# A 16-tile part of a down projection done as pairs of seven quarter products instead of plain blocks

## The chip, the cores and the metric

One core of one Trainium2 chip. The metric is the device time of one execution, in microseconds, median of several. The engines: TensorE (PE in the profile, PEld is its weight load), VectorE (DVE), ScalarE (ACT), GpSimd (POOL), and the queues that issue transfers: SyncE's (SPq) and ScalarE's own (ACTq). TensorE's clock is shown as the granted share of its full speed.

## The reference

The kernel is a decoder block over 512 tokens of width 1024 in float32. The part that matters here is its last stage:

```
xn2 = rms_norm(h, norm2_w)
h = h + (silu(xn2 @ w_ffn_gate) * (xn2 @ w_ffn_up)) @ w_ffn_down     # 1024 -> 2816 -> 1024
y = rms_norm(h, final_norm_w)
```

The last matrix product is the down projection. It sums over 2816 = 22 x 128 features; 128 of them are a row tile of `w_ffn_down`.

## The kernel before, in words

**Arithmetic.** Each float32 operand is split in a high part (a copy rounded to the fp32r format, written by ScalarE) and a low part (operand minus high part, by VectorE or GpSimd). A product is three matmuls: high x high, high x low, low x high.

**Blocks.** The plain form (`block_N`) takes 256 rows of a weight (a block of 1 MB): 4 token tiles x 2 column halves x 2 row tiles x 3 = 48 matmuls with the activations as the 128x128 stationary operand and 512 weight columns as the moving one. ScalarE writes `w_hi` (`high`, `down_high`), GpSimd `w_lo` (`low`), and `raw[s]`, `w_hi[s]`, `w_lo[s]` alternate between two slots. The down projection is eleven such blocks; its activations are split beside it (`act_high` on ScalarE, `act_low` on VectorE). The results add up in all eight PSUM banks, and are added to the residual `h` at the very end (`add_half`), followed by the final norm.

**Pairs.** The gate and up projections of the FFN (all but the first 256 features) run as ten pairs (pair 8 to pair 17 in the numbering of the semaphores; seven pairs of an earlier stage are 1 to 7). A pair multiplies the normed activations by two groups of 128 weight columns each. Both operands are cut in four quarters and seven products of quarters (Winograd's form of Strassen's rule) stand for the eight of the plain form. In order: A11, S1, S2, S3, A12, A22, S4. Each is 2 x 4 x 3 = 24 matmuls with a weight quarter stationary and 256 tokens moving, so a pair is 168 matmuls. A11, A12, A22 are plain weight quarters; S1 to S4 are sums of quarters, formed by VectorE in PSUM banks 4 to 7 (`form_s1` to `form_s4`, in `chain` and `diff`, after ScalarE's `a21_copy`). ScalarE writes all high parts, GpSimd the low parts of A11, A12, A22 (L427), VectorE those of S1 to S4 (L1266). On the other side stand quarters of the activations (x11, x21, x22) and four token sums t1 to t4, formed once. The seven results are put together as they come: `take_p1`, `take_c11` on ScalarE (`taken`), `join_u2`, `join_u3`, `join_c22`, `join_c21`, `join_c12` on VectorE (`joined`). For the FFN, `pair_silu` (ScalarE, L942) and `gated_pair` (GpSimd, L483) then write two tiles of `act`, the input of the down projection.

**What sets the order.** Every engine's program is written out by hand, and engines meet only in semaphores. An engine works its list strictly in order. TensorE waits before each product of pair p for its operand's low part (`s_low`, `plain_low`) and for its bank to be free (`taken`, `joined`). The last join of pair p (`join_c12`) stands in VectorE's list behind `form_s2` of pair p+1, and product S1 of pair p+1 waits for it. SyncE's queue loads the weights of pair p+2 (two transfers of 1 MB) once the quarters of pair p have been read (`pair_read`).

**Seven pairs before.** Pairs 1 to 7 (gates and branches) have the same form. In pairs 3 to 6 the activations themselves change, so their quarters and sums are split again between products (`refill`, `refill_t`, `t_low_of`), and in pairs 5 to 7 GpSimd multiplies by the gates (`weighted`, two instructions). The token sums of the first stage were sent through DRAM (`turned_sums`).

Of the kernel before, what the change touches and what calls it, by code (L numbers as in the profile page):

```python
# [30 lines left out]
P = 128  # L31
SEQ = 512
# [30 lines left out]
HT = SEQ // 2  # L63
DOWN_BLKS = KF // 2


B_DOWN = B_FFN + 2
N_BLKS = B_DOWN + DOWN_BLKS
# [4 lines left out]
LAST_PAIR = MERGE_PAIRS + PAIRS  # L73
SKIPPED_MERGE = 2 * MERGE_PAIRS
SKIPPED = SKIPPED_MERGE + 2 * PAIRS
# [15 lines left out]
def build(nc, x, x_t, wstream, w_lr, cols, vbias, lnw, lnb, sgub, sgu_wt, w_gk2, ident_d, causal_d, finalw, out):  # L91
    with ExitStack() as ctx:
# [7 lines left out]
        def at(p, k, o=0):  # L100
# [49 lines left out]
              [sb("rt_b0", 112, [P, 4, HT]), sb("rt_b1", 116, [P, 4, HT])])  # L150
        raw_out = [sb(f"raw_out{s}", 120 + 16 * s, [P, BLK]) for s in range(2)]
# [11 lines left out]
        op_lo = {n: sb(f"{n}_lo", kb + 4, [P, 2, 4, P], F32R) for n, kb in SLOT.items()}  # L163
        sq_junk0 = sb("sq_junk0", 190, [P, D])
# [46 lines left out]

        turned_sums = nc.dram_tensor("turned_sums", (4, P, 4 * HT), F32).ap()
# [6 lines left out]
        diff = acc[:, 6:8, :].rearrange("p a (k n) -> p a k n", k=4)  # L219

# [53 lines left out]
        h0_low = sem("h0_low")  # L274
        vector_scaled, pool_scaled, scalar_scaled, y_stored = (
# [3 lines left out]
        block = ctx.enter_context(nc.Block())  # L279

# [8 lines left out]
        def _(sp):  # L289
# [86 lines left out]
            with sp.Fori(B_DOWN // 2 + 1, N_BLKS // 2) as i:  # L376
                for s in range(2):
                    sp.wait_ge(hi_ready, i * 2 + (s - 1))
                    sp.wait_ge(lo_ready, i * 2 + (s - 1))
                    sp.dma_start(raw[s][:, :], wstream[bass.ds(i * 2 + (SKIPPED + s), 1)].rearrange("a p n -> (a p) n")  # L380
                                 ).then_inc(raw_landed[s], 16)
# [19 lines left out]
        def _(pool):  # L401
# [23 lines left out]
            def plain(name, c, ks, cs, high):  # L425
                pool.wait_ge(op_high, high)
                pool.tensor_tensor(op_lo[name][:, :, :, :], wp[c][:, :, ks, cs], op_hi[name][:, :, :, :], ALU.subtract  # L427
                                   ).then_inc(plain_low, 1)

            def a11_low(c, high):  # L430
                plain("A11", c, slice(0, 4), slice(0, P), high)

            def a12_low(c, high):
                plain("A12", c, slice(4, 8), slice(0, P), high)

            def a22_low(c, high):
                plain("A22", c, slice(4, 8), slice(P, 2 * P), high)
# [48 lines left out]
            def pair(p, c, first=False, last=False):  # L486

                a12_low(c, at(p, 7, (5 if first else 4) - 7))
                if not first:
                    gated_pair((p[0], p[1] - 1))  # L490
                a22_low(c, at(p, 7, 6 - 7))
                if not last:
                    a11_low(1 - c, at(p, 7, 1))
# [32 lines left out]
            with pool.Fori(1, PAIRS // 2) as i:  # L526
                for c in (1, 0):
                    pair((i, MERGE_PAIRS + 1 - c), c)
            pair((None, LAST_PAIR), 1, last=True)
            pool.wait_ge(product_done, 7 * LAST_PAIR - 3)  # L530
            low(B_DOWN, 0, 8 * B_DOWN)
            gated_pair((None, LAST_PAIR))
            low(B_DOWN + 1, 1, 8 * B_DOWN)
            with pool.Fori(B_DOWN // 2 + 1, N_BLKS // 2) as i:
                for s in range(2):
                    low(i * 2 + s, s, i * 16)
# [14 lines left out]
        def _(a):  # L551
# [1582 lines left out]
```

## Time and profile before

| | |
|---|---|
| median of 3 runs | 826.28 us (825.98 to 826.77) |
| the profiled execution | 826.09 us, of which 824.4 us are its span |
| TensorE busy | 99% of the span, granted clock 0.998 |
| VectorE, ScalarE, GpSimd busy | 62%, 50%, 47% |

The span runs from the first to the last instruction. A matmul's duration in the profile is its way through the pipeline, and several overlap; the time that one adds to a stream is the distance between two starts. Shares of busy time are means over stages with different limits.

### The profile page before, as it was taken

Reading aid. Unit: us, or ns where it says so; the run is one execution under the profiler, and the core shown is the slowest. Engines: PE = TensorE matmul, PEld = TensorE weight load, DVE = VectorE, ACT = ScalarE, POOL = GpSimd, SP = SyncE. Lnnn points to the kernel's source line nnn. Section 1 sums busy time; section 2 is a strip of 40 time slices with the busy share of each in tenths; the row PEclk is TensorE's granted clock in tenths of the full one; section 3 lists DMA queues with packets and bytes.
Section 4 is the critical chain, followed back from the end, with each engine's and each line's share of the span. In section 5 each row is a group of like instructions: output and inputs, shape, how many; then the busy total and the mean of one; then the engine's idle time right before and its main releaser. Section 6 shows DMA issues by size and latency. Waiting matters only on the chain.

```text
span 824.4 us, 12835 instructions
## 1 busy us (share of the span) xinstructions
PE 816.0 (99%) x5224; PEld 742.7 (90%) x5224; DVE 509.7 (62%) x506; ACT 414.9 (50%) x464; POOL 383.7 (47%) x129
## 2 busy tenths in 40 slices
PE   9999999999999999999999999999999999999996
PEld 7888888888888899999998899999999999888885
DVE  6477377374675867888863387666666666244444
ACT  4523446665675645856432674555544445122234
POOL 4445424424224533568954433444444445544443
PEclk9999999999999999999999999999999999999999
DMA  9842422121123353333252305433333321322212
GB/s 339 309 163 103 157 98 103 53 101 66 56 89 127 96 181 103 103 104 103 103 194 117 103 2 164 144 102 102 102 102 102 102 102 52 127 102 79 81 44 102
DMA packets 20615, 94.36 MB, mean 114 GB/s; under 512 B 1889, under 2 KB 2273, under 8 KB 15585
## 3 DMA queue, kind: packets, MB, share of 16 engines
q1 hardware_dynamic: 17456, 83.92, 29.6%
q10 hardware_dynamic: 3120, 9.90, 3.1%
q8 instruction: 28, 0.46, 0.2%
q14 instruction: 11, 0.08, 0.0%
HBM read 89.62 MB, written 4.19 MB: 114 GB/s over the span
## 4 chain that ended last, share of the span: by engine, by line
PE 99%; DVE 0%; ACT 0%; issue 0%; ACTq 0%
PE acc L1847 14%; PE acc L1849 14%; PE acc L1850 14%; PE acc L1641 9%; PE acc L1643 9%; PE acc L1642 9%; PE acc L1624 7%; PE acc L1625 6%; PE acc L1626 6%; PE acc L1667 3%; PE acc L1761 1%; PE acc L1800 1%; PE acc L1805 1%; PE acc L1792 1%; PE acc L1657 1%; PE acc L1974 0%
## 5 line engine op out<-in xcount | busy, mean ns | idle before, releaser
L406 POOL TENSOR_TENSOR w_lo<-raw,w_hi 128x2048 fp32r<-128x2048 f32 x34 | 158.8, 4671 | 219.6 <-ACT w_hi L560 219.6
L427 POOL TENSOR_TENSOR A_lo<-wp,A_hi 128x1024 fp32r<-128x1024 f32 x51 | 126.2, 2474 | 143.1 <-ACT A_hi L732 143.1
L560 ACT ACTIVATE w_hi<-raw 128x2048 fp32r<-128x2048 f32 x34 | 64.9, 1912 | 125.6 <-PE acc L1643 111.3
L1849 PE MATMUL acc<-xt_lo,A_hi 128*128 128x256 f32 x408 | 115.5, 283 | 0.0
L1850 PE MATMUL acc<-xt_hi,A_lo 128*128 128x256 f32 x408 | 115.5, 283 | 0.0
L1847 PE MATMUL acc<-xt_hi,A_hi 128*128 128x256 f32 x408 | 115.5, 283 | 0.0
L745 ACT ACTIVATE S_hi<-acc 128x1024 fp32r<-128x1024 f32 x68 | 68.1, 1024 | 88.6 <-PE acc L1850 55.6
L1266 DVE TENSOR_TENSOR S_lo<-acc,S_hi 128x1024 fp32r<-128x1024 f32 x68 | 81.8, 1220 | 18.6 <-ACT S_hi L745 18.6
L1624 PE MATMUL acc<-xt_hi,w_hi 128*128 128x512 f32 (+1 forms) x240 | 92.5, 385 | 0.0
L1626 PE MATMUL acc<-xt_hi,w_lo 128*128 128x512 f32 (+1 forms) x240 | 91.7, 382 | 0.0
L1625 PE MATMUL acc<-xt_lo,w_hi 128*128 128x512 f32 (+1 forms) x240 | 91.7, 382 | 0.0
L1527 DVE TENSOR_TENSOR al<-act,ah 128x1024 fp32r<-128x1024 f32 x11 | 48.2, 4385 | 63.0 <-ACT ah L957 63.0
L1849 PEld LDWEIGHTS acc<-xt_lo,A_hi 128*128 128x128 f32 x408 | 78.3, 192 | 0.0
L1847 PEld LDWEIGHTS acc<-xt_hi,A_hi 128*128 128x128 f32 x408 | 78.3, 192 | 0.0
L1850 PEld LDWEIGHTS acc<-xt_hi,A_lo 128*128 128x128 f32 x408 | 78.3, 192 | 0.0
L1641 PE MATMUL acc<-w_hi,ah 128*128 128x512 f32 x176 | 68.5, 389 | 0.0
L1642 PE MATMUL acc<-w_lo,ah 128*128 128x512 f32 x176 | 68.5, 389 | 0.0
L1643 PE MATMUL acc<-w_hi,al 128*128 128x512 f32 x176 | 68.5, 389 | 0.0
L1847 PE MATMUL acc<-tb_hi,S_hi 128*128 128x256 f32 x240 | 67.9, 283 | 0.0
L1849 PE MATMUL acc<-tb_lo,S_hi 128*128 128x256 f32 x240 | 67.9, 283 | 0.0
L1850 PE MATMUL acc<-tb_hi,S_lo 128*128 128x256 f32 x240 | 67.9, 283 | 0.0
L732 ACT ACTIVATE A_hi<-wp 128x1024 fp32r<-128x1024 f32 x51 | 53.8, 1055 | 18.7 <-PE acc L1850 18.7
(284 smaller groups left out, 2030.2 us busy)
## 6 DMA issues: line engine op xcount, KB each, us to landing
raw<-wstream SPq DMA_DIRECT2D x34, 1024.0 KB, 4.8
wp<-wstream SPq DMA_DIRECT2D x34, 1024.0 KB, 8.3
turned_sums<-tx ACTq DMA_DIRECT2D x4, 512.0 KB, 3.8
raw_out<-wstream SPq DMA_DIRECT2D x2, 1024.0 KB, 5.8
raw_ffn<-wstream SPq DMA_DIRECT2D x2, 1024.0 KB, 9.1
h<-x ACTq DMA_DIRECT2D x1, 2048.0 KB, 14.1
xw<-x_t SPq DMA_DIRECT2D x3, 512.0 KB, 10.1
mt_raw<-turned_sums SPq DMA_DIRECT2D x3, 512.0 KB, 4.1
```

The lines of the kernel that those rows point to most:

```text
L406: pool.tensor_tensor(w_lo[s][:, :], raw[s][:, :], w_hi[s][:, :], ALU.subtract).then_inc(lo_ready, 1)
L427: pool.tensor_tensor(op_lo[name][:, :, :, :], wp[c][:, :, ks, cs], op_hi[name][:, :, :, :], ALU.subtract).then_inc(plain_low, 1)
L1266: v.tensor_tensor(op_lo[name][:, :, :, :], src, op_hi[name][:, :, :, :], ALU.subtract).then_inc(s_low, 1)
L1624: pe.matmul(dst, wh[:, k, cs], rh[:, k, ts], start=(k == 0), stop=False)
L1625: pe.matmul(dst, wh[:, k, cs], rl[:, k, ts], start=False, stop=False)
L1626: last = pe.matmul(dst, wl[:, k, cs], rh[:, k, ts], start=False, stop=(k == KD - 1))
L1641: pe.matmul(dst, lh[:, k, ts], wh[:, k, cs], start=(first and k == 0), stop=False)
L1642: pe.matmul(dst, lh[:, k, ts], wl[:, k, cs], start=False, stop=False)
L1643: mm = pe.matmul(dst, ll[:, k, ts], wh[:, k, cs], start=False, stop=(last and k == 1))
L1847: pe.matmul(dst, wh[:, g, k, :], x[0][:, k, :], start=(start and g == 0 and k == 0), stop=False, skip_group_check=True)
L1849: pe.matmul(dst, wh[:, g, k, :], x[1][:, k, :], start=False, stop=False, skip_group_check=True)
L1850: mm = pe.matmul(dst, wl[:, g, k, :], x[0][:, k, :], start=False, stop=(k == 3), skip_group_check=True)
```

## The change

The first 16 of the 22 row tiles of the down projection (act tiles 0 to 15) become four pairs, 18 to 21, ahead of three remaining plain blocks. Two pairs share a chunk of eight row tiles: pairs 18 and 19 take chunk 0, each for one half of the 1024 output columns, pairs 20 and 21 chunk 1. Here the activations are stationary (128x128) and a quarter of the weight is moving, 256 columns wide (`down_product`).

- The token sums of each chunk (four of 512 KB) are formed by VectorE during pairs 13 to 16 (`act_sums`), stored to DRAM by ScalarE's queue (`store_sums`), and read back by SyncE's queue during pair 17 and pair 19 (`sum_back`) into the place that their low parts will take. They lie meanwhile in tiles of `act` that pairs 15 to 17 will fill, so GpSimd waits for the stores (`t_stored`) ahead of its lists for pairs 16 and 17.
- During pairs 17/18 and 19/20 the split quarters and sums are replaced by those of the next chunk: seven instructions on ScalarE (`act_x`, `act_t`), five on GpSimd (`act_x`, `act_t_low`) and two on VectorE (`act_t_low_of`), of 1024 elements a partition each.
- The four joined quarters of a down pair go to `dq`, and GpSimd adds them to `h` (`add_pair`, two instructions a pair).
- Weight loads of a down pair are four transfers of 512 KB in pieces of 2 KB.
- The loops over pairs are written out from pair 13 on.

```diff
+DOWN_CHUNKS = 2
+DOWN_PAIRS = 2 * DOWN_CHUNKS
+K_PLAIN = KD * DOWN_CHUNKS
...
+PLAIN_BLKS = DOWN_BLKS - K_PLAIN // 2
...
-LAST_PAIR = MERGE_PAIRS + PAIRS
+LAST_FFN = MERGE_PAIRS + PAIRS
+LAST_PAIR = LAST_FFN + DOWN_PAIRS
...
+SUM_TILES = (20, 18, 16, 18), (18, 20, 20, 18)
+SUM_ORDER = (0, 1, 2, 3), (0, 2, 1, 3)
+FIRST_SUMS = 6
...
-            for q in range(2, PAIRS):
-                pair_read((None, MERGE_PAIRS + q - 1))
-                pair_weights(wstream[W_FFN + 2 * q + 2:W_FFN + 2 * q + 4], q % 2)
+            def sum_back(p, n):
+                m = (p - LAST_FFN) // 2
+                dst = sum_raw[n][:, :, :].rearrange("p k t -> p (k t)") if n < 3 else sum_raw[n]
+                src = down_sums[4 * m + n] if n < 3 else down_sums[4 * m + n].rearrange("p (k t) -> p k t", k=4)
+                sp.wait_ge(t_stored, A_STORED + 64 * (m + 1))
+                sp.wait_ge(product_done, 7 * p + (2, 3, 4, 6)[n] - 7)
+                sp.dma_start(dst, src).then_inc(sum_landed[n], 16)
+
+            def down_weights(p):
+                c, m, n = p % 2, (p - LAST_FFN - 1) // 2, (p - LAST_FFN - 1) % 2
+                for hf, landed in enumerate((k1_landed[c], k2_landed[c])):
+                    for j in range(2):
+                        k = 4 * hf + 2 * j
+                        sp.dma_start(wd[c][:, k:k + 2, :], wstream[W_DOWN + 4 * m + k // 2].rearrange("p (k n) -> p k n", k=2)
+                                     [:, :, n * HALF:(n + 1) * HALF]).then_inc(landed, 16)
+
+            for p in range(MERGE_PAIRS + 3, LAST_PAIR + 1):
+                ends = p - 2 in (LAST_FFN, LAST_FFN + 2)
+                if ends:
+                    for n in range(3):
+                        sum_back(p - 2, n)
+                pair_read((None, p - 2))
+                if p <= LAST_FFN:
+                    w = W_FFN + 2 * (p - MERGE_PAIRS)
+                    pair_weights(wstream[w:w + 2], p % 2)
+                else:
+                    down_weights(p)
+                if ends:
+                    sum_back(p - 2, 3)
             pair_read((None, LAST_PAIR - 1))
             for s in range(2):
                 sp.dma_start(raw[s][:, :], wstream[B_DOWN + SKIPPED + s]).then_inc(raw_landed[s], 16)
...
+            def add_pair(p, halves=(0, 1)):
+
+                pool.wait_ge(joined, 5 * p)
+                pool.wait_ge(taken, 2 * p)
+                n = (p - LAST_FFN - 1) % 2
+                for i in halves:
+                    c0 = n * HALF + i * HT
+                    quarter = h[:, :, c0:c0 + HT]
+                    pool.tensor_tensor(quarter, quarter, dq[(p - LAST_FFN - 1) % 2][:, 2 * i:2 * i + 2, :, :].rearrange("p j t c -> p (j t) c"),
+                                       ALU.add).then_inc(h_added, 1)
...
+            for p in range(MERGE_PAIRS + FIRST_SUMS, LAST_FFN + 1):
+                if p - 1 >= MERGE_PAIRS + 8:
+                    pool.wait_ge(t_stored, A_STORED + 64 * (p - 1 - MERGE_PAIRS - 7))
+                pair((None, p), p % 2)
+            for p in range(LAST_FFN + 1, LAST_PAIR + 1):
+                down_pair(p)
             pool.wait_ge(product_done, 7 * LAST_PAIR - 3)
...
+            def store_sums(q):
+                m = (q - FIRST_SUMS) // 2
+                for i in range(2):
+                    i += 2 * ((q - FIRST_SUMS) % 2)
+                    n = SUM_ORDER[m][i]
+                    a.wait_ge(t_formed, A_FORMED + 4 * m + i + 1)
+                    a.dma_start(down_sums[4 * m + n], act_sum[SUM_TILES[m][n]][:, :, :].rearrange("p k t -> p (k t)")
+                                ).then_inc(t_stored, 16)
+
+            def act_x(p, product, m, ks, ts):
+                a.wait_ge(product_done, 7 * p + product - 7)
+                k = KD * m + ks.start
+                a.activation(xt_hi[:, ks, ts], act[:, k:k + 4, ts], ACT.Copy).then_inc(refill_high, 1)
+
+            def act_t(p, n):
+                a.wait_ge(sum_landed[n], 16 * ((p - LAST_FFN) // 2 + 1))
+                a.wait_ge(product_done, 7 * p + (2, 3, 4, 6)[n] - 7)
+                dst = tb_hi[n][:, :, :] if n < 3 else xt_hi[:, 0:4, HT:SEQ]
+                a.activation(dst, sum_raw[n][:, :, :], ACT.Copy).then_inc(t_high, 1)
...
+            def act_sums(q):
+
+                m = (q - FIRST_SUMS) // 2
+                x11, x12, x21, x22 = act_quarters(m)
+                t1, t2, t3, t4 = (act_sum[k][:, :, :] for k in SUM_TILES[m])
+                if q == FIRST_SUMS:
+                    v.wait_ge(pair_ready, 3)
+                    v.tensor_tensor(t1, x12, x11, ALU.subtract).then_inc(t_formed, 1)
+                    v.wait_ge(t_formed, A_FORMED + 1)
+                    v.tensor_tensor(t2, x22, t1, ALU.subtract).then_inc(t_formed, 1)
...
+                if q == FIRST_SUMS + 3:
+                    v.wait_ge(t_formed, A_FORMED + 5)
+                    v.wait_ge(t_stored, A_STORED + 64 + 32)
+                    v.tensor_tensor(t2, x22, t1, ALU.subtract).then_inc(t_formed, 1)
+                    v.wait_ge(t_formed, A_FORMED + 7)
+                    v.tensor_tensor(t4, x21, t2, ALU.subtract).then_inc(t_formed, 1)
...
+            def down_product(name, x, b, start):
+
+                wh, wl = row_hi[name], row_lo[name]
+                for t in range(2):
+                    dst = bank[b][:, t * HT:(t + 1) * HT]
+                    ts = slice(t * P, (t + 1) * P)
+                    for k in range(4):
+                        pe.matmul(dst, x[0][:, k, ts], wh[:, k, :], start=(start and t == 0 and k == 0), stop=False,
+                                  skip_group_check=True)
+                        pe.matmul(dst, x[0][:, k, ts], wl[:, k, :], start=False, stop=False, skip_group_check=True)
+                        mm = pe.matmul(dst, x[1][:, k, ts], wh[:, k, :], start=False, stop=(k == 3),
+                                       skip_group_check=True)
+                mm.then_inc(product_done, 1)
```

On GpSimd, before: its rows for pair 17 (the last pair then; A_lo is a plain quarter's low part, act the gated tiles of pair 16 and then 17) and the start of the blocks.

```order
L427 TENSOR_TENSOR A_lo<-wp_120,A_hi 128x1024 [waits op_high]
L483 TENSOR_TENSOR act<-silp,cq 128x1024 [waits silp_ready]
L427 TENSOR_TENSOR A_lo<-wp_120,A_hi 128x1024 [waits op_high]
L406 TENSOR_TENSOR w_lo_53<-raw_49,w_hi_51 128x2048 [waits hi_ready,raw_landed0,product_done]
L483 TENSOR_TENSOR act<-silp,cq 128x1024 [waits silp_ready]
```

On GpSimd, after: its rows for pair 17 (the first six) and pair 18 (A_row_lo is a plain quarter of a down pair, xt_lo and tb_lo are quarters and sums of the activations).

```order
L490 TENSOR_TENSOR A_lo<-wp_129,A_hi 128x1024 [waits op_high,t_stored]
L552 TENSOR_TENSOR xt_lo<-act,xt_hi 128x4x256 [waits refill_high]
L546 TENSOR_TENSOR act<-silp,cq 128x1024 [waits silp_ready]
L490 TENSOR_TENSOR A_lo<-wp_129,A_hi 128x1024 [waits op_high]
L490 TENSOR_TENSOR A_row_lo<-wd_144,A_row_hi 128x1024 [waits op_high]
L557 TENSOR_TENSOR tb_lo_127<-sum_raw_111,tb_hi_124 128x1024 [waits t_high]
L490 TENSOR_TENSOR A_row_lo<-wd_144,A_row_hi 128x1024 [waits op_high]
L552 TENSOR_TENSOR xt_lo<-act,xt_hi 128x4x256 [waits refill_high]
L546 TENSOR_TENSOR act<-silp,cq 128x1024 [waits silp_ready,t_stored]
```

Pair 17 had three instructions of 1024 elements here and now has six, and the first of them waits for the stores too.

On VectorE, before: its rows for pair 17 (acc is chain or diff, u and cq are joins, al the activations' low part for the blocks).

```order
L1259 TENSOR_TENSOR acc<-acc,wp_120 128x1024
L1508 TENSOR_TENSOR cq<-acc,u_82 128x512 [waits product_done]
...
L1505 TENSOR_TENSOR u_83<-acc,u_82 128x512 [waits joined,product_done]
L1508 TENSOR_TENSOR cq<-acc,u_83 128x512 [waits joined,pair_ready]
L1527 TENSOR_TENSOR al_146<-act,ah_144 128x1024 [waits ah_ready]
L1508 TENSOR_TENSOR cq<-acc,u_82 128x512 [waits product_done] x2
```

On VectorE, after: its rows from `join_c22` of pair 17 to `form_s2` of pair 18.

```order
L1703 TENSOR_TENSOR cq<-acc,u_83 128x512 [waits joined,pair_ready]
L1754 TENSOR_TENSOR tb_lo_125<-sum_raw_109,tb_hi_122 128x1024 [waits t_high]
L1447 TENSOR_TENSOR acc<-wd_144,acc 128x1024
L1754 TENSOR_TENSOR tb_lo_126<-sum_raw_110,tb_hi_123 128x1024 [waits t_high]
L1703 TENSOR_TENSOR cq<-acc,u_82 128x512 [waits product_done]
L1461 TENSOR_TENSOR S_row_lo<-acc,S_row_hi 128x1024 [waits op_high]
L1703 TENSOR_TENSOR cq<-acc,u_82 128x512 [waits product_done,s_low]
L1451 TENSOR_TENSOR acc<-acc,wd_144 128x1024
```

Two splits of sums (L1754) stand ahead of `join_c21`, and `join_c12` of pair 17 now stands ahead of `form_s2`, behind the low part of S1.

## Rows read from the trace of the kernel before

**Rows 1.** The page: busy time by engine, and the chain that ended last.

```profile
PE 816.0 (99%) x5224; PEld 742.7 (90%) x5224; DVE 509.7 (62%) x506; ACT 414.9 (50%) x464; POOL 383.7 (47%) x129
...
PE 99%; DVE 0%; ACT 0%; issue 0%; ACTq 0%
```

**Rows 2.** Timeline of PE (start us, duration us): first of pair 8, pair 17, blocks; last.

```profile
496.44 0.28 PE L1847 MATMUL acc<-xt_hi,A_hi 128*128 128x256 f32 x1
...
677.88 0.28 PE L1847 MATMUL acc<-xt_hi,A_hi 128*128 128x256 f32 x1
...
698.03 0.40 PE L1641 MATMUL acc<-w_hi,ah 128*128 128x512 f32 x1
...
817.52 0.39 PE L1643 MATMUL acc<-w_hi,al 128*128 128x512 f32 x1
```

**Rows 3.** Timeline of PE, an earlier stage: weights stationary, 512 columns moving.

```profile
284.49 0.39 PE L1625 MATMUL acc<-xt_lo,w_hi 128*128 128x512 f32 x1
284.72 0.39 PE L1626 MATMUL acc<-xt_hi,w_lo 128*128 128x512 f32 x1
```

**Rows 4.** Timeline of DVE, pairs 16 and 17.

```profile
671.59 1.22 DVE L1256 TENSOR_TENSOR acc<-wp,acc 128x1024 f32<-128x1024 f32 x1
675.20 0.69 DVE L1508 TENSOR_TENSOR cq<-acc,u 128x512 f32<-128x512 f32 x1 [2.39 <-PE acc L1850]
...
679.74 0.68 DVE L1508 TENSOR_TENSOR cq<-acc,u 128x512 f32<-128x512 f32 x1
...
690.84 0.69 DVE L1508 TENSOR_TENSOR cq<-acc,u 128x512 f32<-128x512 f32 x1
691.45 4.93 DVE L1527 TENSOR_TENSOR al<-act,ah 128x1024 fp32r<-128x1024 f32 x1
```

**Rows 5.** Timeline of POOL, pair 17.

```profile
678.24 2.41 POOL L427 TENSOR_TENSOR A_lo<-wp,A_hi 128x1024 fp32r<-128x1024 f32 x1 [6.20 <-ACT A_hi L732]
682.58 2.42 POOL L483 TENSOR_TENSOR act<-silp,cq 128x1024 f32<-128x1024 f32 x1 [1.93 <-ACT silp L942]
...
690.66 4.63 POOL L406 TENSOR_TENSOR w_lo<-raw,w_hi 128x2048 fp32r<-128x2048 f32 x1 [3.27 <-ACT w_hi L560]
```

**Rows 6.** Timeline of ACT, end of pair 16 and pair 17.

```profile
677.10 1.06 ACT L732 ACTIVATE A_hi<-wp 128x1024 fp32r<-128x1024 f32 x1
679.94 1.02 ACT L745 ACTIVATE S_hi<-acc 128x1024 fp32r<-128x1024 f32 x1 [1.78 <-DVE acc L1259]
680.96 0.60 ACT L948 ACTIVATE p<-acc 128x512 f32<-128x512 f32 x1
681.45 1.05 ACT L942 ACTIVATE silp<-cq 128x1024 f32<-128x1024 f32 x1
```

**Rows 7.** Timeline of POOL, pair 6, where activations are replaced.

```profile
388.58 2.42 POOL L453 TENSOR_TENSOR xt_lo<-yb,xt_hi 128x1024 fp32r<-128x1024 f32 x1
390.93 5.79 POOL L449 TENSOR_TENSOR sg_a<-mcq,sg_a 128x1024 f32<-128x1024 f32 x2
396.66 3.41 POOL L427 TENSOR_TENSOR A_lo<-wp,A_hi 128x1024 fp32r<-128x1024 f32 x1
```

**Rows 8.** Timeline of DVE in pair 6.

```profile
395.38 2.42 DVE L1316 TENSOR_TENSOR xt_lo<-yb,xt_hi 128x1024 fp32r<-128x1024 f32 x1
```

**Rows 9.** Transfers: issues (count, KB each, median us to landing), then sums stored and read.

```profile
wp<-wstream SPq DMA_DIRECT2D x34, 1024.0 KB, 8.3
turned_sums<-tx ACTq DMA_DIRECT2D x4, 512.0 KB, 3.8
mt_raw<-turned_sums SPq DMA_DIRECT2D x3, 512.0 KB, 4.1
xn_in<-x SPq DMA_DIRECT2D x2, 512.0 KB, 12.5
...
DMA to landing us min/median/max: 2.6/4.0/7.1
```

**Rows 10.** Timeline of SPq in pair 15: the issue of the weights of pair 17.

```profile
647.52 0.88 SPq L316 DMA_DIRECT2D wp<-wstream  x2
```

More of the change, by code:

```diff
@@ L969, in pair @@
                 a22_high(c, n)
+                a.wait_ge(product_done, at(p, 7, 3 - 7))
+                s_high("S4", chain, at(p, 4))
+                a.wait_ge(s_low, at(p, 4, 1 - 4))
+                a21_copy(1 - c, nn, rows)
+                a11_high(1 - c, nn, rows)
+                if renewed is not None:
+                    act_t(p[1], 0)
+                take_c11(p, first)
+                if renewed is not None:
+                    act_t(p[1], 1)
+                    act_x(p[1], 5, renewed, slice(4, 8), slice(0, HT))
+                    act_t(p[1], 2)
@@ new lines, in pair @@
+                a.wait_ge(product_done, at(p, 7, 6 - 7))
+                s_high("S1", chain, at(p, 4, 1), rows)
+                s_high("S3", diff, at(p, 4, 2), rows)
+                a12_high(1 - c, nn, rows)
+                if q is not None and q < PAIRS:
+                    store_sums(q)
+            def store_sums(q):
[6 more added lines that the diff above has]
+                                ).then_inc(t_stored, 16)
@@ L1550, in pair @@
                 join_c22(p, first)
+                if q == PAIRS:
+                    act_t_low_of(0, 0)
+                form_s3(1 - c, rows)
+                if q == PAIRS:
+                    act_t_low_of(0, 1)
+                elif q is not None:
+                    act_sums(q)
+                join_c21(p)
+                s_low_of("S1", chain, at(p, 7, 2), rows)
+                if q != PAIRS:
+                    s_low_of("S3", diff, at(p, 7, 3), rows)
+                v.wait_ge(s_low, at(p, 4, 1))
@@ L1551, in pair @@
                 if last:
                     act_low(1, 1)
-                if not last:
-                    form_s3(1 - c)
-                join_c21(p)
-                if not last:
-                    s_low_of("S1", chain, at(p, 7, 2))
-                    s_low_of("S3", diff, at(p, 7, 3))
-                    v.wait_ge(s_low, at(p, 4, 1))
+                else:
+                    form_s3(1 - c, True)
+                if ends:
+                    act_t_low_of(m + 1, 1)
+                down_c21(p)
@@ L1561, in _ @@
+                if not last:
+                    s_low_of("S1", chain, 7 * p + 2, True)
+                    if not ends:
+                        s_low_of("S3", diff, 7 * p + 3, True)
+                    v.wait_ge(s_low, 4 * p + 1)
             pair((None, MERGE_PAIRS + 1), 0, 16, first=True)
-            with v.Fori(1, PAIRS // 2) as i:
+            with v.Fori(1, (FIRST_SUMS - 1) // 2 + 1) as i:
                 pair((i, MERGE_PAIRS), 1, i * 16 + 16)
                 pair((i, MERGE_PAIRS + 1), 0, i * 16 + 16)
-            pair((None, LAST_PAIR), 1, 0, last=True)
@@ L1566, in _ @@
-            join_c12((None, LAST_PAIR))
+            for q in range(FIRST_SUMS, PAIRS + 1):
+                pair((None, MERGE_PAIRS + q), (q - 1) % 2, 16 * (q // 2 + 1) + 16 * (q == PAIRS), q=q)
+            for p in range(LAST_FFN + 1, LAST_PAIR + 1):
+                down_pair(p)
+            down_c12(LAST_PAIR)
             act_low(2, 0)
-            with v.Fori(0, 4) as i:
-                for s in range(2):
-                    act_low(i * 2 + (3 + s), 1 - s)
             v.wait_ge(fw_landed, 16)
+            v.wait_ge(h_added, 2 * DOWN_PAIRS)
@@ L2036, in down @@
+            for p in range(LAST_FFN + 1, LAST_PAIR + 1):
+                down_pair(p)
             def down(m, s, first=False, last=False):
```

345 lines of the change are left out of this document (263 added, 82 removed).

## The prediction, made before the changed kernel was run

> **What bounds the kernel now.** I read the page's busy times first: PE is busy in 99% of the span, and the chain that ended last lies on PE for 99% [rows 1]. Next the timeline of PE, for the distance between starts. Ten pairs of 168 matmuls run from 496.44 to 698.03 us [rows 2]: 201.59 us, so 20.159 us a pair, 2.880 us a product and 0.1200 us for a matmul of 256 columns. The 528 matmuls of the down projection start from 698.03 to 817.52 [rows 2]: 527 steps in 119.49 us, 0.2267 us for one of 512 columns. Neither stretch leaves room for a wait, so every other engine is hidden here, and the stage is worth what its matmuls are worth. Then I read VectorE, GpSimd and ScalarE inside pair 17, since this is the work that has to stay hidden. Below, "+x" is x us after a pair's first matmul (677.88 for pair 17).
>
> **Matmuls.** Removed: eight blocks of 48 = 384 matmuls of 512 columns, 384 x 0.2267 = 87.1 us. Added: four pairs of 168 = 672 matmuls of 256 columns, 672 x 0.1200 = 80.6 us. The difference is 6.4 us, not the 10.9 us that an eighth of 87.1 would be, because two short matmuls take 0.0133 us longer than one long one (2 x 0.1200 - 0.2267). What is new is which operand stands still. With the weights stationary and 512 columns moving the starts lie 0.23 us apart [rows 3], as with the activations stationary in the blocks [rows 2]; so the side does not matter at 512 columns, and I take 0.1200 at 256. Bounds: 0.1133 (half of the long one), a gain of 10.9 us, and 0.1333 (the fixed 0.0133 us of each matmul twice over), a loss of 2.5 us. Neither end has a row that supports it.
>
> The first row also tests a rule. The rows give 0.1200 and 0.2267 us. The Trainium skill, page "TensorE: Matmul & The Clock Gate", section "Back-to-back issue gap", gives for one stream at the full clock N columns over 2.4 GHz plus about 2.5 ns: 109.2 and 215.8 ns. By the page the sum would be an estimated 82.9 - 73.4 = 9.5 us of gain; this trace doesn't agree with it at either width (11 ns more each), and the measurement decides.
>
> **Work that is added behind TensorE.** One VectorE instruction of 1024 elements costs 1.22 us [rows 4], one of GpSimd 2.41 [rows 5], one of ScalarE 1.05 [rows 6].
> - Token sums, pairs 13 to 16: two VectorE instructions a pair, behind `form_s3`. In pair 16 that ends at 672.81, and the next instruction starts at 675.20 after 2.39 us idle [rows 4]; two take 2.4. Nothing is moved.
> - Pair 17, GpSimd: six instructions of 1024 elements (14.5 us) in 20.2. Their order matters. A12's low part starts at +0.36 today [rows 5], x11's at about +4.7 (ScalarE is done with `take_p1` at +3.6 and needs 1.05 for its high part [rows 6]), then `gated_pair` and A22's low part: +11.9. Product A22 starts at +14.40. The slack is 2.5 us.
> - But the first of them now waits for two stores. ScalarE issues them beside or behind the copy of 677.10 [rows 6], at -0.8 to +0.3. Landing was 2.6 to 7.1 us, median 3.8 for a store [rows 9]. So X, the time at which GpSimd may begin, is +1.8 to +7.7, likeliest +3.4 to +4.5. Four instructions in a row end at X + 9.6, so TensorE waits for A22 only if X is over 4.8: 0 to 2.9 us, and at the likeliest X nothing.
> - Pair 19, GpSimd: x11 at +4.7, `add_pair` twice, A22: four instructions in a row, +14.3 against +14.40. This is the tightest place. A precedent is pair 6: four instructions from 388.58 end at 400.07 [rows 7], with seven in the pair, and no wait of PE on it. I take 0.1, from nothing to 1.2 (one more instruction of VectorE ahead of it).
> - Pair 18 carries seven instructions (16.9 us) and its A22 and last refill have over 0.9 us each; pairs 20 and 21 carry less before product A22.
> - VectorE, pairs 17 and 19: two splits of sums (2.4 us) between `join_c22` (start 690.84, +12.96 [rows 4]) and `join_c21` (+17.3). With `form_s3` that is 3.7 us from +13.6: +17.3. Nothing is lost if they run at once; the lock below decides.
> - ScalarE: 3 to 4 extra instructions in pair 17 and 19, in idle time; S1's high part moves from +17.4 to about +17.9, its low part to about +20.1; product S1 of the next pair needs it at +23.04.
> - `join_c12` of pairs 17 and 19 ahead of `form_s2`: it comes earlier than the +1.86 to +2.54 of today [rows 4], S2's low part follows at about +5; S2 starts at +5.76.
> - Transfers. SyncE issues weights at 647.52, +10.0 of pair 15 [rows 10], and they land in 8.3 us [rows 9]; needed is the first half at about +9.9 of the next pair, 20 us later. The queue now waits for products 2 to 4 (+11.5 at the latest) first, and the 512 KB of sums land in 4.1 us [rows 9] at about +9.9, +12.8, +15.7; ScalarE takes them at +11.9, +15, +17. Late by 2 us they still cost nothing. The weights of pair 19 are issued latest (+14.5 of pair 17, behind A22's low part); their pieces of 2 KB are new, and if these took twice the 8.3 us they would land at +31.1 where +30.1 is wanted: 1 us, at most.
> - Last three blocks: GpSimd has the first `w_lo` by +18.3 of pair 21, the second by +26.6 (needed +31), the third by +38 (needed +42). The final `add_half` sees every addition long done. The tail stays.
>
> Sum: -6.4 for matmuls, +0.2 for waits of a tenth at two or three places: -6.2. The profiled execution (826.09, 1.7 over its span of 824.4) would become 819.9; its 826.09 is 0.2 below the median of 826.28, so the median becomes **820.1 us**.
>
> **Rivals.**
> 1. The lock between VectorE and GpSimd delays a join (20%). A VectorE instruction with both inputs in SBUF took 4.93 us at 691.45, and ended 1.1 us after GpSimd's of 690.66 (4.63 us) [rows 4, 5]; in pair 6 such a one took 2.42 and GpSimd's next 3.41 instead of 2.41 [rows 7, 8]. So whoever comes second waits, for up to 2.4 us (VectorE) or 1.1 (GpSimd). In pair 17 with X between about 3.6 and 4.0 each split of a sum meets a GpSimd instruction that has just begun: `join_c21` ends at +22.1, S1's low part at +23.3, `join_c12` at +24.0 where TensorE wants it at +23.04, and S2 is 0.7 late behind it: 1.7 us. Twice that (pair 19 too), or with X late as well, makes 1.5 to 4.5 us: 821.6 to 824.6. For it: all three places are within 1 us of their limit. Against it: pairs 3 to 6 had the same forms, and PE's stream kept its pace.
>    The Trainium skill, page "SBUF — State Buffer", section "SBUF: two separate sides", says that the shared pair of ports is an exclusive lock for a whole instruction, taken by VectorE with two SBUF inputs against a reading GpSimd. By that rule the trace agrees (4.93 for 1.22).
> 2. Slower than before: the sums come back late (4%). `act_t` for t3 stands in ScalarE's list ahead of S1, S3 and A12 of the next pair, and everything waits if the load is late. Issued at +11.6, it must land by about +19.2 (7.6 us) for `join_c12` to stay in time, and each further us is lost twice (pairs 17 and 19). Slower by 0.2% needs 8.1 us of loss, so 11.7 us of landing each. For it: 512 KB once took 12.5 [rows 9]. Against it: that was at the start with the queues full; sums took 2.6 to 7.1 [rows 9].
> 3. A matmul with 256 weight columns moving has a longer step than 0.1200 (3%): from 0.1296 us on the gain is gone, and at 0.1333 it is 828.8. Against it: rows 2 and 3 at 512 columns.
> 4. Matmuls at 0.1133, or a pace that is better with weights moving (2%): 815.4 at best.
> 5. Several losses of 1 and 2 together, 4.8 to 8.0 us (4%): 824.9 to 828, no change that can be told.
>
> **How the numbers follow.** Forecast 67% (819.4 to 821.5), rival 1 20%, rival 2 4%, rival 3 3%, rival 4 2%, rest 4%. The range for 8 in 10 takes the forecast's own range and rival 1 up to 3.5 us of waits: 819.0 to 823.6. Faster by over 0.2% (below 824.6) is 67 + 20 + 2 = 89%, less 1 for rival 1's upper end: 88%. Within 0.2% (about what runs of this kernel can tell): rival 5 and half of rival 3, with that 1: 6%. Slower: 6%.
>
> **What would show it.** PE's starts 0.1200 us apart in the 672 new matmuls, and 80.6 to 81.5 us from the first of pair 18 to the first block's; three blocks in 32.6 us. If I am wrong, PE's timeline has gaps in pair 17 ahead of A22 (a late store), at S1 or S2 of pairs 18 and 20 (the lock, with VectorE's L1754 at 2 us or more each), or at A22 of pair 19. Pairs 8 to 16 keep 20.16 us. If the gap between starts is itself longer, rival 3 holds; if ScalarE idles ahead of its splits of sums on a DMA for microseconds, rival 2.

## The result and the profile after

The changed kernel takes 820.24 us in the median of six executions (819.95 to 820.39), the kernel before beside it 826.14 (825.97 to 826.77, six): a ratio of 0.9926, 95% interval 0.9917 to 0.9936. Forecast were 820.1 in a range of 819.0 to 823.6. The profiled execution took 820.24, of which 818.5 are its span, at a granted clock of 0.999.

The page, busy times and chain that ended last; these two lines answer to [rows 1].

```profile
PE 810.3 (99%) x5512; PEld 752.0 (92%) x5512; DVE 539.6 (66%) x562; ACT 440.8 (54%) x502; POOL 421.0 (51%) x151
...
PE 99%; DVE 0%; ACT 0%; issue 0%; ACTq 0%
```

TensorE has 288 matmuls more (672 for 384) and is busy 5.7 us less. VectorE has 30 us more work, ScalarE 26, GpSimd 37, and the chain still lies on TensorE.

The timeline of PE answers to [rows 2]: first matmul of pairs 8, 17 and 18, the two on either side of the only gap, first and last of the blocks.

```profile
496.89 0.28 PE L2137 MATMUL acc<-xt_hi,A_hi 128*128 128x256 f32 x1
...
678.33 0.28 PE L2137 MATMUL acc<-xt_hi,A_hi 128*128 128x256 f32 x1
...
698.49 0.28 PE L2333 MATMUL acc<-A_row_hi,xt_hi 128*128 128x256 f32 x1
...
733.04 0.34 PE L2333 MATMUL acc<-A_row_hi,xt_hi 128*128 128x256 f32 x1
733.23 0.28 PE L2335 MATMUL acc<-A_row_lo,xt_hi 128*128 128x256 f32 x1
...
779.18 0.40 PE L1931 MATMUL acc<-w_hi,ah 128*128 128x512 f32 x1
...
811.62 0.39 PE L1933 MATMUL acc<-w_hi,al 128*128 128x512 f32 x1
```

From pair 8 to pair 17 there are 181.44 us in both traces. Pairs 18 to 21 take 779.18 - 698.49 = 80.69 us, which is 672 x 0.1200 (80.64) and one gap: between 733.04 and 733.23 lie 0.19 us instead of 0.12. (A step is the distance between two starts.) The three blocks have 143 steps in 32.44 us, 0.2269 each. From pair 8's first matmul to the last matmul there are 314.73 us, and there were 321.08 [rows 2]: 6.35 less. The last matmul is 6.9 us from the span's end in both. Pair 8 starts 0.45 us later than in the trace before; what lies ahead of it is unchanged, and in the other traces below that start lies anywhere from 496.51 to 497.19. So 6.35 is the effect in the two traces. The 5.90 between the two medians is less, and the scatter of the start can account for it, which is argued and not shown; the four variants below without a gap worth naming came out 6.1 to 6.4 under the kernel before beside them.

GpSimd in pairs 17, 18 and 19, answering to [rows 5].

```profile
680.19 2.42 POOL L490 TENSOR_TENSOR A_lo<-wp,A_hi 128x1024 fp32r<-128x1024 f32 x1 [7.79 <-DMA down_sums<-act_sum]
...
687.76 2.41 POOL L490 TENSOR_TENSOR A_lo<-wp,A_hi 128x1024 fp32r<-128x1024 f32 x1
...
725.81 4.76 POOL L567 TENSOR_TENSOR h<-h,dq 128x1024 f32<-128x1024 f32 x2
730.53 5.78 POOL L490 TENSOR_TENSOR A_row_lo<-wd,A_row_hi 128x1024 fp32r<-128x1024 f32 x2
```

In pair 17 GpSimd was held by the store, as the releaser says, and began at 680.19, +1.86 (678.24, +0.36, before [rows 5]). A22's low part ends at 690.17, +11.8, with 2.6 us in hand. In pair 19 the row of 730.53 holds two splits: the first, of 2.4 us, ends at about 732.9 = +14.3, and that is the gap of 0.07 us at the product A22, whose first matmuls with the low part stand in the rows of PE above.

Why the store was early: VectorE forming the last two sums, then ScalarE and its queue at the end of pair 16.

```profile
673.35 1.22 DVE L1748 TENSOR_TENSOR act_sum<-act,act_sum 128x1024 f32<-128x1024 f32 x1
674.61 1.22 DVE L1750 TENSOR_TENSOR act_sum<-act,act_sum 128x1024 f32<-128x1024 f32 x1
...
675.65 1.02 ACT L861 ACTIVATE S_hi<-acc 128x1024 fp32r<-128x1024 f32 x1 [2.28 <-PE acc L2140]
675.66 0.81 ACTq L1114 DMA_DIRECT2D down_sums<-act_sum  x2
...
677.47 1.06 ACT L846 ACTIVATE A_hi<-wp 128x1024 fp32r<-128x1024 f32 x1
```

In ScalarE's list the stores stand behind three copies, of which 675.65 is the first and 677.47 the last. They were issued as the first began, at -2.7, instead of the -0.8 to +0.3 of the forecast. The first of the two had its own wait met at 674.57, when its sum was formed, and still went out only at 675.66, when the copy at the head of the list had its product from TensorE. So the stores were held by the waits ahead of them in the list, and not by the copies' work (experiment 4 shows the same once more). That an engine works its list strictly in order, as said above, holds for a transfer only in this sense.

VectorE in pairs 17, 18 and 19, answering to [rows 4]: the splits of sums are L1754, the joins L1703 and L1798.

```profile
692.02 1.64 DVE L1754 TENSOR_TENSOR tb_lo<-sum_raw,tb_hi 128x1024 fp32r<-128x1024 f32 x1
...
694.72 1.21 DVE L1754 TENSOR_TENSOR tb_lo<-sum_raw,tb_hi 128x1024 fp32r<-128x1024 f32 x1
...
697.31 1.23 DVE L1461 TENSOR_TENSOR S_row_lo<-acc,S_row_hi 128x1024 fp32r<-128x1024 f32 x1 [0.78 <-ACT S_row_hi L861]
698.76 0.69 DVE L1703 TENSOR_TENSOR cq<-acc,u 128x512 f32<-128x512 f32 x1 [0.22 <-PE acc L2140]
...
732.34 1.69 DVE L1754 TENSOR_TENSOR tb_lo<-sum_raw,tb_hi 128x1024 fp32r<-128x1024 f32 x1
...
735.09 2.31 DVE L1754 TENSOR_TENSOR tb_lo<-sum_raw,tb_hi 128x1024 fp32r<-128x1024 f32 x1
...
739.16 0.69 DVE L1798 TENSOR_TENSOR dq<-acc,u 128x512 f32<-128x512 f32 x1
```

`join_c12` starts at 698.76 (+20.4) and 739.16 (+20.5); TensorE wants it done by +23.04. Three of the four splits took 1.64 to 2.31 us where 1.21 is the time of one alone. Each of the three ended 1.1 us after the GpSimd instruction beside it (at 692.58, 732.9 and 736.3), as in [rows 4, 5], and the reserve took it up.

Transfers on the page, and the reads of the sums and the weights' issue in pair 17 on SyncE's queue; they answer to [rows 9, 10].

```profile
wd<-wstream SPq DMA_DIRECT2D x16, 512.0 KB, 6.4
down_sums<-act_sum ACTq DMA_DIRECT2D x8, 512.0 KB, 3.4
sum_raw<-down_sums SPq DMA_DIRECT2D x8, 512.0 KB, 3.3
```
```profile
684.33 6.08 SPq L419 DMA_DIRECT2D sum_raw<-down_sums  x3
690.51 2.53 SPq L426 DMA_DIRECT2D wd<-wstream  x4
```

The 2 KB pieces cost TensorE nothing: a `wd` load lands in 6.4 us. (512 KB of sums land in 3.3, but they are not issued four in a row, so what the pieces cost the transfer is not shown.) Each issues in about 0.6 us, so the last of the four leaves at about 692.5, and the first half is wanted at about 708.4 (+30.1 of pair 17).

### The profile page after: what moved, and what is told of

It reads as the page before. It is cut to its first block, busy times and chain, and to the rows that moved or that the text cites. A ratio compares the mean times of both kernels' runs of the same rounds, so it can differ in the third digit from the quotient of the medians.

```text
span 818.5 us, 13393 instructions
## 1 busy us (share of the span) xinstructions
PE 810.3 (99%) x5512; PEld 752.0 (92%) x5512; DVE 539.6 (66%) x562; ACT 440.8 (54%) x502; POOL 421.0 (51%) x151
## 4 chain that ended last, share of the span: by engine, by line
PE 99%; DVE 0%; ACT 0%; issue 0%; ACTq 0%
PE acc L2137 14%; PE acc L2139 14%; PE acc L2140 14%; PE acc L1914 7%; PE acc L1916 6%; PE acc L1915 6%; PE acc L1933 6%; PE acc L1931 6%; PE acc L1932 6%; PE acc L2333 3%; PE acc L2335 3%; PE acc L2336 3%; PE acc L1957 3%; PE acc L2051 1%; PE acc L2090 1%; PE acc L2095 1%
## 5 line engine op out<-in xcount | busy, mean ns | idle before, releaser
L469 POOL TENSOR_TENSOR w_lo<-raw,w_hi 128x2048 fp32r<-128x2048 f32 x26 | 122.2, 4701 | 165.6 <-ACT w_hi L674 165.6
L861 ACT ACTIVATE S_hi<-acc 128x1024 fp32r<-128x1024 f32 x68 | 68.1, 1024 | 89.5 <-PE acc L2140 56.3
L674 ACT ACTIVATE w_hi<-raw 128x2048 fp32r<-128x2048 f32 x26 | 49.6, 1910 | 68.3 <-PE acc L1933 53.6
L846 ACT ACTIVATE A_hi<-wp 128x1024 fp32r<-128x1024 f32 x51 | 53.8, 1055 | 17.9 <-PE acc L2140 17.9
L1916 PEld LDWEIGHTS acc<-xt_hi,w_lo 128*128 128x128 f32 x240 | 45.1, 188 | 8.8
L1914 PEld LDWEIGHTS acc<-xt_hi,w_hi 128*128 128x128 f32 x240 | 45.1, 188 | 8.7
L1915 PEld LDWEIGHTS acc<-xt_lo,w_hi 128*128 128x128 f32 x240 | 45.1, 188 | 8.5
L2137 PE MATMUL acc<-mt_hi,S_hi 128*128 128x256 f32 x168 | 47.7, 284 | 0.0
```

Source lines behind the costliest of these rows:

```text
L469: pool.tensor_tensor(w_lo[s][:, :], raw[s][:, :], w_hi[s][:, :], ALU.subtract).then_inc(lo_ready, 1)
L674: a.activation(w_hi[s][:, :], raw[s][:, :], ACT.Copy).then_inc(hi_ready, 1)
L846: a.activation(high_of(name, rows), weights_of(name, c, rows), ACT.Copy).then_inc(op_high, 1)
L861: a.activation(high_of(name, rows), src, ACT.Copy).then_inc(op_high, 1)
L1914: pe.matmul(dst, wh[:, k, cs], rh[:, k, ts], start=(k == 0), stop=False)
L1915: pe.matmul(dst, wh[:, k, cs], rl[:, k, ts], start=False, stop=False)
```

## The experiments

Ten kernels, in three groups, each group on one chip beside the kernel before. The forecast had said what a matmul costs, where the added work has no slack, and how much it has elsewhere; each is tried alone. All compute the reference in full.

**1. One chunk of the two** (one_chunk): two pairs and seven plain blocks.

```
-DOWN_CHUNKS = 2
+DOWN_CHUNKS = 1
```

The rest of its edit, not shown, is what follows from it: four more blocks in each engine's loops, and in pair 19 both additions to `h` ahead of A22's low part as before, with no exchange of activations there.

> Half the change: only the first eight row tiles as two pairs (18 and 19), seven plain blocks behind them. If the gain is matmuls alone (192 of 512 columns at 0.2267 us out, 336 of 256 at 0.1200 in), it is half of the whole change's: -3.2 us on the kernel before, 822.9 us. If the whole change also lost something at its second exchange of activations (pairs 19 and 20) or gained from elsewhere, the half is not half: under 822.5 or over 823.5.

Timeline of PE, first matmul of pair 8 and the last one.

```profile
496.64 0.28 PE L2139 MATMUL acc<-xt_hi,A_hi 128*128 128x256 f32 x1
...
814.52 0.39 PE L1935 MATMUL acc<-w_hi,al 128*128 128x512 f32 x1
```

317.88 us for 321.08: 3.20 less, half of 6.40, and no gap. In the trace the gain belongs to the pairs, in proportion. The median is 823.67 (823.12 to 823.90, six), ratio 0.9968 [0.9956, 0.9981], 2.5 us less. That is over the 823.5 above which the expectation called the half not a half. The profiled execution, 823.12, was the shortest of the six and comes out 3.0 under the kernel before; the three longest (823.74 to 823.90) have a mean granted clock of 0.997, the others 0.998 to 0.999. What they lost no trace shows, so the half is shown for the matmuls and not for the median.

**2. The kernel before with blocks of short matmuls** (blocks256): each matmul of the eleven down blocks as two of 256 columns, nothing else.

```
-                block_N(s, ah[s], al[s], first, last, free)
+                narrow_block(s, ah[s], al[s], first, last, free)
```

`narrow_block`, not shown, is `block_N` with an inner loop over the two 256-column parts of each 512 columns.

> The kernel before, with each matmul of the down projection's eleven blocks cut in two of 256 columns (1056 instead of 528), activations stationary. If the step is 0.0133 us plus 256 columns at the full clock, 1056 x 0.1200 = 126.7 us for 119.7: +7.0 us, 833.1 us. By a fixed part of 2.5 ns (the Trainium skill's page on TensorE) an estimated +1.3 us. If activations stationary with narrow weights are slower than 0.1200, more than +7.

Timeline of PE: first of the blocks, last.

```profile
698.12 0.28 PE L2046 MATMUL acc<-w_hi,ah 128*128 128x256 f32 x1
...
824.72 0.28 PE L2049 MATMUL acc<-w_hi,al 128*128 128x256 f32 x1
```

Median 833.17 (832.97 to 833.19, four), ratio 1.0082 [1.0065, 1.0099]; 1055 steps in 126.60 us, 0.1200 each, 7.1 us more than the 119.49 of 527 long steps [rows 2]. So a short matmul with the activations stationary and the weights moving costs 0.1200 as well, and the 0.0133 us by which two short ones exceed a long one is what separates the gain of 6.4 from the 10.9 of an eighth. The Trainium skill's rule that the forecast weighed ("TensorE: Matmul & The Clock Gate", "Back-to-back issue gap"; the section calls it the gap of an isolated matmul) would make this about 528 x (2 x 109.2 - 215.8) = 1.4 us, an estimate from the page; the measurement says 7.1.

**3. The stores behind the copies** (store_after_copy): ScalarE issues pair 16's two stores only when the last copy of that pair is done.

```
+                    if q == PAIRS - 1:
+                        a.wait_ge(op_high, 7 * LAST_FFN - 3)
```

> The changed kernel; the last two stores of sums wait for A12's copy of pair 17 to end, so GpSimd starts its list of pair 17 some 2.9 us later, at about +4.8 instead of +1.96. Four instructions of 2.4 us end at +14.35; TensorE wants A22 at +14.40. Theory (slack 2.8 us): 0 to +0.1 us, 820.2 to 820.3. If the lock with VectorE bites in this position: +1 to +2.

Timeline of GpSimd, pair 17.

```profile
682.46 2.41 POOL L490 TENSOR_TENSOR A_lo<-wp,A_hi 128x1024 fp32r<-128x1024 f32 x1 [10.21 <-DMA down_sums<-act_sum]
...
691.94 3.39 POOL L490 TENSOR_TENSOR A_row_lo<-wd,A_row_hi 128x1024 fp32r<-128x1024 f32 x1
```

GpSimd starts at +4.3, about 2.4 us later than in the changed kernel and within the forecast's likeliest +3.4 to +4.5; +4.8 was expected of this run. A22's low part ends at 691.97; the next split, behind it, takes 3.39 us for 2.41 beside VectorE's. TensorE has no gap, not even in pair 19, whose list is unchanged: the 0.07 us there are as small as what differs from trace to trace. 820.0 us (819.87 to 820.28, four), 0.9924 [0.9907, 0.9940].

**4. The stores still later** (store_after_p1): issued behind `take_p1` of pair 17.

```
+                if q == PAIRS:
+                    store_sums(PAIRS - 1)
...
-                if q is not None and q < PAIRS:
+                if q is not None and q < PAIRS - 1:
                     store_sums(q)
```

> The changed kernel; these two stores come behind take_p1 of pair 17, so GpSimd starts at about +8.2. Theory (each us past +4.8 stops TensorE for one): A22's low part at +17.8, +3.4 us, 823.6 us, in one gap of PE in front of product A22 of pair 17. If the list of pair 17 had other slack: under +2. If the lock adds to it at the following join: over +4.5.

Timelines of ScalarE and its queue, GpSimd and PE in pair 17 (the copy at 681.41 is `take_p1`).

```profile
681.41 0.60 ACT L1064 ACTIVATE p<-acc 128x512 f32<-128x512 f32 x1
681.42 0.81 ACTq L1116 DMA_DIRECT2D down_sums<-act_sum  x2
```
```profile
685.44 2.40 POOL L490 TENSOR_TENSOR A_lo<-wp,A_hi 128x1024 fp32r<-128x1024 f32 x1 [13.01 <-DMA down_sums<-act_sum]
```
```profile
692.61 0.28 PE L2142 MATMUL acc<-xt_hi,A_lo 128*128 128x256 f32 x1
695.05 0.38 PE L2139 MATMUL acc<-xt_hi,A_hi 128*128 128x256 f32 x1 [2.16 <-POOL A_lo L490]
```

GpSimd may begin at +7.1; the forecast's slack ended at +4.8, which makes 2.3 us, and the gap ahead of A22 is 695.05 - 692.61 - 0.12 = 2.32. The start of +8.2 and the loss of 3.4 that were expected of this run were too much, for the same reason as in the forecast: the stores were issued as `take_p1` began and not when it was done. Median 823.2 (822.41 to 824.33, six), 0.9966 [0.9953, 0.9978]; the profiled execution took 822.63.

**5 and 6. The sums read back one product later, and two** (sums_1_later, sums_2_later).

```
-                sp.wait_ge(product_done, 7 * p + (2, 3, 4, 6)[n] - 7)
+                sp.wait_ge(product_done, 7 * p + (3, 4, 5, 7)[n] - 7)
```

That is sums_1_later; sums_2_later has `(4, 5, 6, 8)[n]` in its place.

> The changed kernel; each read of a sum from DRAM waits for one product more (2.88 us later). ScalarE takes t3's sum about 1 us later, S1's low part and the join behind it still come in time. Theory (transfers have slack): no change, 820.2 +- 0.2. If the round trip through DRAM is what TensorE nearly waits for: +1 to +5.

> The changed kernel; each read of a sum waits for two products more (5.76 us later). Worked out: t3 lands at +20.7, S1's low part at +23.95, the join of C12 at +24.6 where +23.04 is wanted (1.6 us), S2's low part 0.6 us late behind it: 2.2 us in each of pairs 17/18 and 19/20, +4.4 us, 824.6 us. If only the landing mattered and the list behind it did not: 0.

One product later costs nothing: 820.0 (819.94 to 820.42, four), 0.9924 [0.9908, 0.9941]. Two products later: 825.23 (824.50 to 826.66, ten), 0.9988 [0.9979, 0.9998]. Timelines of PE, DVE and ACT at the first of its four gaps (the last row is the copy of t3's sum).

```profile
700.89 0.28 PE L2336 MATMUL acc<-A_row_hi,xt_lo 128*128 128x256 f32 x1
702.73 0.35 PE L2333 MATMUL acc<-S_row_hi,tb_hi 128*128 128x256 f32 x1 [1.56 <-DVE S_row_lo L1461]
```
```profile
700.68 1.23 DVE L1461 TENSOR_TENSOR S_row_lo<-acc,S_row_hi 128x1024 fp32r<-128x1024 f32 x1 [1.88 <-ACT S_row_hi L861]
```
```profile
698.67 1.06 ACT L1126 ACTIVATE tb_hi<-sum_raw 128x1024 fp32r<-128x1024 f32 x1 [0.78 <-DMA sum_raw<-down_sums]
```

1.72 us at S1 and 0.52 at S2 in pair 18, 1.88 and 0.54 in pair 20, 5.0 in all with the first steps behind them; 1.6, 0.6 and 4.4 in all were expected. TensorE waits for S1's low part and then for the join behind it: the copies of the sums stand ahead of S1's copy in ScalarE's list. A delay of 5.76 us cost 2.5 a chunk, so the slack of the reads is about 3.3 us.

**7 and 8. One more GpSimd instruction in pair 19, and in pair 20** (extra19, extra20).

```
             def act_x(n, m, ks, ts):
                 pool.wait_ge(refill_high, A_REFILL + n)
+                if n == 4:
+                    pool.tensor_tensor(silp[:, :, :], xt_hi[:, 0:4, 0:HT], xt_hi[:, 0:4, 0:HT], ALU.subtract)
```

That is extra19; extra20 has `n == 5`. The result goes to memory that nobody reads.

> The changed kernel with one more GpSimd instruction of 1024 elements (2.41 us, into unused memory) in pair 19 ahead of the additions to h. Theory: the list of pair 19 has no slack, so TensorE waits 2.3 us before product A22: 822.5 us. If the wait of 0.07 us seen there came from elsewhere: 820.2.

> The same instruction in pair 20, whose list reaches A22 with 4.9 us to spare. Theory: no change, 820.2 +- 0.2. If GpSimd's total load in this stage sets the pace: +1 to +2.4.

In pair 20 it costs nothing (820.15, 820.01 to 820.69, four). In pair 19 it costs 4.1 us, where 2.3 were expected: 824.37 (822.96 to 824.82, seven), 0.9971 [0.9959, 0.9982]. Timelines of GpSimd, VectorE and PE in pair 19 of extra19.

```profile
723.75 1.89 POOL L552 TENSOR_TENSOR silp<-xt_hi 128x1024 f32<-128x1024 f32 x1 [2.10 <-ACT xt_hi L1122]
...
732.67 6.72 POOL L490 TENSOR_TENSOR A_row_lo<-wd,A_row_hi 128x1024 fp32r<-128x1024 f32 x2
```
```profile
732.64 1.22 DVE L1756 TENSOR_TENSOR tb_lo<-sum_raw,tb_hi 128x1024 fp32r<-128x1024 f32 x1
```
```profile
733.23 0.28 PE L2338 MATMUL acc<-A_row_hi,xt_lo 128*128 128x256 f32 x1
736.12 0.39 PE L2335 MATMUL acc<-A_row_hi,xt_hi 128*128 128x256 f32 x1 [2.61 <-POOL A_row_lo L490]
```

The gap is 2.77 us: 0.07 and the 1.89, and 0.8 more, because VectorE's split began at 732.64, a moment ahead of GpSimd's of 732.67, which was over only at about 736.0. That is rival 1's lock, with a price, at the place that has no slack. The rest of the 4.1 us is not a wait. Stretches of PE in extra19: us, then busy us and count of PE, PEld, DVE, ACT and POOL, granted clock, share of DMA, GB/s.

```profile
733.30:736.10 2.80, 0.21 (x2) 0.01 (x1) 2.68 (x3) 2.55 (x4) 2.80 (x2) 1.00 0.01 4
736.10:737.60 1.50, 1.48 (x12) 1.48 (x13) 1.05 (x1) 0.88 (x1) 1.50 (x1) 1.00 0.11 16
737.60:741.10 3.50, 3.50 (x19) 3.50 (x19) 0.61 (x1) 0.61 (x1) 3.50 (x2) 0.51 0.89 301
741.10:750.00 8.90, 8.90 (x76) 8.90 (x76) 6.71 (x7) 4.37 (x6) 5.41 (x3) 1.00 0.50 173
```

After the gap TensorE ran 1.5 us at full clock, then 3.5 us at a granted 0.51, the level of 1.2 GHz: steps of 0.214 us, about 1.5 us lost.

**9. Half of that instruction** (extra19_half): 512 elements instead of 1024, in pair 19.

> Pair 19 gets a GpSimd instruction half as long as in extra19 (512 elements instead of 1024, about 1.0 us instead of 1.89) in the same place ahead of A22's low part; everything is still computed, the extra instruction writes memory that nobody reads. In the changed kernel TensorE waits 0.07 us there. My theory: the wait becomes 0.07 + 1.0 = 1.1 us, or about 2.1 if VectorE's split of a sum takes its turn first, as it did in extra19, and the clock stays at its full level because the wait is shorter than the 2.8 us after which it fell: 821.2 to 822.3 us, all executions within 0.3 us of each other. Rival: any wait of a microsecond or more brings the half clock, so some executions show 15 steps of 0.214 us behind the wait and are 1.5 us longer (822.7 to 823.8). Second rival: the half clock in extra19 had nothing to do with the wait; then it is missing here and the times lie close, which by itself does not tell this one from my theory.

Timelines of GpSimd and PE in pair 19.

```profile
723.53 1.04 POOL L552 TENSOR_TENSOR silp<-xt_hi 128x512 f32<-128x512 f32 x1 [2.10 <-ACT xt_hi L1122]
```
```profile
733.01 0.28 PE L2338 MATMUL acc<-A_row_hi,xt_lo 128*128 128x256 f32 x1
734.09 0.39 PE L2335 MATMUL acc<-A_row_hi,xt_hi 128*128 128x256 f32 x1 [0.80 <-POOL A_row_lo L490]
```

1.04 us of GpSimd make a gap of 0.96 and 0.10 on the next step, so nothing hides it. Here VectorE's split did not come first. All steps behind the gap are 0.120 us. 821.28 us (820.89 to 821.46, four), 1.0 above the changed kernel, 0.9939 [0.9922, 0.9955]; the four lie 0.6 apart, where 0.3 was expected.

**10. One addition moved behind A22** (add_split19): in pair 19 the second half of pair 18's quarter is added to `h` behind A22's low part.

```
-                    add_pair(p - 1)
+                    add_pair(p - 1, (0,))
                     a22_low(c, 7 * p - 1, rows=True)
+                    add_pair(p - 1, (1,))
```

> Nothing is left out. In pair 19 the second half of the addition of pair 18's quarter to h is done behind A22's low part instead of ahead of it, so that low part starts 2.4 us earlier. The wait of 0.07 us of TensorE at A22 of pair 19 should vanish, and pairs 18 to 21 take 80.64 us from the first matmul of pair 18 to the block's, the pure 672 steps of 0.1200. Time 820.1 to 820.2, which the median can't tell from 820.24. Rival: the order is now such that the half addition, later, meets VectorE's splits of sums, and join_c12 or A11's low part comes late: a gap of 0.5 to 1.5 us at S1 or S2 of pair 20.

Timelines of PE (first matmul of pair 18, first of the blocks) and of GpSimd (A22's low part in pair 19).

```profile
698.11 0.28 PE L2334 MATMUL acc<-A_row_hi,xt_hi 128*128 128x256 f32 x1
...
778.75 0.40 PE L1932 MATMUL acc<-w_hi,ah 128*128 128x512 f32 x1
```
```profile
727.81 2.41 POOL L490 TENSOR_TENSOR A_row_lo<-wd,A_row_hi 128x1024 fp32r<-128x1024 f32 x1
```

80.64 us, the bare 672 steps, and no gap from pair 8 to the end. A22's low part ends at 730.22, 2.8 us ahead of its product. 819.91 us (819.79 to 820.32, four), 0.9925 [0.9908, 0.9941]: the place with no slack is gone, for a gain that the median can't tell.

## Why the prediction was right

The sum holds in its trace: forecast were -6.4 for matmuls and +0.2 for waits, measured -6.42 and +0.07.

- **Matmuls: right.** 672 steps of 0.1200 (pairs 18 to 21), 0.2269 in the blocks. That the operands change sides costs nothing (experiment 2), and in the trace half the pairs give half the gain (experiment 1). Rivals 3 and 4 are out.
- **Pair 19: right to a tenth.** Forecast was a low part at +14.3 and a wait of 0.1; it came at +14.3, with 0.07. Experiments 7 to 10 show that this place has nothing in hand: a microsecond added there is a microsecond lost, in pair 20 it is free, and with one addition fewer ahead of it the low part has 2.8 us to spare. The 0.07 itself is at the size of what traces differ by (none in experiment 3).
- **GpSimd in pair 17: the slack right, the start mis-sized.** The step "ScalarE issues them beside or behind the copy of 677.10" took the list's order for the order in time. The issue waits for the waits of the copies ahead of it in the list, not until these copies are done, and the start was +1.9, not +3.4 to +4.5, near the lower bound. That the forecast of no wait held in spite of it is not luck: it allowed for starts up to +4.8. The limit of +4.8 is right: at +4.3 (experiment 3) no wait, at +7.1 one of 2.32 us (experiment 4).
- **VectorE and the lock (rival 1): mechanism right, no loss.** Splits of 1.64 to 2.31 us are in the trace, but S1's low part ends at +20.2, where about +20.1 was forecast without the lock, and the join behind it, over at +21.1, has two microseconds in reserve. The window of +3.6 to +4.0 in which the rival put a loss of 1.7 us was hit in no trace, so that loss is neither shown nor ruled out: the starts nearest to it, +3.1 (extra19_half, where the first split took 2.35 us) and +4.3 (experiment 3, where the second took 2.09), had none. In the traces here the lock cost TensorE time only in extra19, at A22 of pair 19, a place at which I had not looked for it.
- **Sums by way of DRAM (rival 2): right that it is slack.** They land in 3.3 us, forecast 4.1. The forecast let t3's sum land up to +19.2 for the join in front of S1. In experiment 6 it came at +20.7 (698.67) and TensorE waited 1.72 us at S1, which puts that limit at +19.0. S2's wait behind it makes the slack smaller than the join alone has: about 3.3 us on the reads. The chain (copies of the sums, S1's copy, its split, the join) is the one it named.
- **ScalarE, transfers, tail: right.** No wait lies there.

## What to carry over

Where one engine is busy for 99% with evenly spaced instructions, a change is worth its count times the distance of starts, taken for each width from the trace: two short matmuls take longer than one of twice the width (here by 0.0133 us), which took 4.5 of 10.9 us. Then walk each hidden engine's list between two deadlines, and add up instructions one by one; here that found the place with no slack to a tenth of a microsecond. A DMA that stands behind copies in an engine's list may be issued before they run, so bound its time by when its own waits and those ahead of it in the list are met, not by when the copies are done.

## What was not expected of the hardware

A gap can cost more than its length. Behind 2.77 us of TensorE's idleness (extra19) the granted clock went to 0.51 from 737.6 to 741.1, having been 1.00 before, across the gap and for 1.5 us behind it. In that kernel two executions took 822.96 and 823.10 us at a mean clock of 0.999, the other five 824.2 to 824.8 at 0.995 to 0.997, so it is not there every time. Behind the gap of 2.32 us (store_after_p1) the profiled execution kept its clock (822.63 us, 0.998), but three of six show 0.996 and 823.6 to 824.3. With gaps of 1.72 and 1.88 us (sums_2_later) the profiled one kept it too, and three of ten show 0.996 and 825.8 to 826.7. Behind 0.96 us (extra19_half) none of four does, and no execution of a kernel without a gap shows less than 0.997. Only the fall in extra19 was seen in a trace. For the others it is argued from their mean clock, and that the gap is its cause is argued from these counts.
